# Cumulated forget logarithms as two rows of the forget attention's queries and keys; modulation sums two units earlier

## The chip, the cores and the metric

One core of one Trainium2 chip. The metric is the device time of one launch in microseconds (us); times of the kernel before are the median of several runs. One more execution was taken with the hardware profiler; all views come from that one.

## What is computed

Two transformer blocks, one after the other, on 256 tokens of width 1024 in float32. The first puts 16 meta tokens ahead (272 in all), and runs a SwiGLU feed-forward, a mixer of two attentions with 8 heads each, and a second feed-forward. The second block (modulated by a vector `c`) runs a gated linear attention beside a convolution, and then a layer that picks 16 of 16384 experts for each token and head and adds up their rows. The change lies in the second attention of the first block, the forget attention:

```python
def block_causal_attention(q, k, v, scale, key_valid, cum=None):
    ...
        s = jnp.einsum('bqhd,bkhd->bhqk', q[:, q0:q1], k[:, :q1]) * scale
        if cum is not None:
            cq = jnp.transpose(cum[:, q0:q1], (0, 2, 1))[:, :, :, None]
            ck = jnp.transpose(cum[:, :q1], (0, 2, 1))[:, :, None, :]
            s = s + (cq - ck)
    ...
    fq = rms_norm(fq[:, :, 0], g_q_fox)
    fk = rms_norm(fk[:, :, 0], g_k_fox)
    log_f = jax.nn.log_sigmoid(f_logit + b_forget)
    cum = jnp.cumsum(log_f, axis=1)
    o_fox = block_causal_attention(fq, fk, fv, 1.0 / math.sqrt(FOX_HEAD_DIM), key_valid, cum)
```

So the score of query t and key s of a head is scale * (q_t . k_s) + cum_t - cum_s. The second block needs its modulation vector, `silu(c) @ ada_w + ada_b`, a product with a matrix of 1024 x 6144.

## The kernel before

Each engine runs its own program in order, tied to the others by semaphores. SyncE (SP) loads the stream of weights in pieces of 1 MB into a ring of four (`load`, L578), loads the modulation matrix in 32 parts of 768 KB (`load_ada`, L585), and between them copies the experts' two tables side by side into one (`pair_up`, L592: two DRAM to DRAM copies of 512 KB a block, 128 blocks). `load_ada` waits until VectorE has done the sum two before it. 24 blocks are copied right after the last piece ahead of the second feed-forward; the last eight modulation loads come then, each followed by one block.

The modulation product is made by VectorE, in 32 sums `ada_add` (L1149, the work is L1153) of 128x1536. The last eight (parts 6 and 7 of `kt`) lie in the attention loop.

The mixer's projections end near 287 us. From then to 341 us the heads' queries and keys are normalised and rotated. The forget attention's queries lie in `fqz`, 128 rows for each of 8 heads, where an even head has its 64 rows in rows 0 to 63 and an odd one in rows 64 to 127; the other half is zero from a memset of VectorE (L1232). Its keys `fk` lie in pairs, two heads in 128 rows, so that a query with zeros in the other half picks its own. The forget logarithms of all heads lie in rows 96 to 103; VectorE cumulates them with a scan into `cumz` (L1283), zero in the other rows (L1229), and negates it into `ncumz` (L1285).

The attention runs over 32 units: 8 latent heads and then 8 forget heads, each in two tiles t of 128 queries. An even unit sees 144 keys (narrow), an odd one 272 (wide). TensorE works in the order `scores_of(n+2)`, `turn_probs(n)`, `weigh(n-1)`. In a forget unit `scores_of` has four products into one bank: queries and keys (L2006), `cumz` with a column of the constant `sel` that picks the head and divides by the scale (L2008), the same column with `ncumz` (L2009), and the causal mask (L2010). VectorE works in the order `soft_max(n+1)` (row maximum L1291, negated and scaled L1293), `scale_p(n)` (L1300, L1302), and behind every odd unit from 17 to 31 one `ada_add`. ScalarE does the exponential (L853), the copy of turned probabilities `probs_out(n-2)` (L767, L769) and the copy of the output `head_out(n-3)` (L777). Then comes the output product (L2056), a norm, the first half of the modulation sums' totals on TensorE (L1841), and the second feed-forward.

GpSimd splits weights for the feed-forwards (L666) and has nothing to do from 275 to 445 us.

Of the kernel before, what the change touches and what calls it, by code (L numbers as in the profile page):

```python
# [23 lines left out]
ALU = mybir.AluOpType  # L24
AX_X = mybir.AxisListType.X

P = 128
# [66 lines left out]
for _name, _n in VECS:  # L94
# [6 lines left out]
          ("ones", P), ("rot", P), ("cos", T), ("sin", T), ("neg_mask", P), ("iota", TOPK), ("sel", HEADS)]  # L101
# [9 lines left out]
def constants():  # L111
    c = np.zeros((P, N_CONSTS), np.float32)

    def put(name, a):
        at = CON[name][0]
        c[:a.shape[0], at:at + a.shape[1]] = a

    put("ident", np.eye(P, dtype=np.float32))
    for name, n in (("mean_d", D), ("mean_256", 256), ("mean_128", 128)):
        put(name, np.full((P, P), 1.0 / n, np.float32))  # L120
    put("mean_96", np.full((QK, QK), 1.0 / QK, np.float32))
    put("mean_64", np.kron(np.eye(2), np.full((HD, HD), 1.0 / HD)).astype(np.float32))
    put("ones", np.ones((P, P), np.float32))
    half = ROPE // 2
    rot = np.zeros((QK, QK), np.float32)
    for i in range(half):
        rot[NOPE + half + i, NOPE + i] = -1.0
        rot[NOPE + i, NOPE + half + i] = 1.0
    put("rot", rot)
    freq = (1.0 / (np.float32(10000.0) ** (np.arange(half, dtype=np.float32) / np.float32(half)))).astype(np.float32)  # L130
    ang = (np.arange(T, dtype=np.float32)[None, :] * freq[:, None]).astype(np.float32).astype(np.float64)
    cos = np.ones((QK, T), np.float32)
    sin = np.zeros((QK, T), np.float32)
    for at in (NOPE, NOPE + half):
        cos[at:at + half] = np.cos(ang)
        sin[at:at + half] = np.sin(ang)
    put("cos", cos)
    put("sin", sin)
    put("neg_mask", np.where(np.arange(P)[None, :] > np.arange(P)[:, None], NEG, 0.0).astype(np.float32))
    sel = np.zeros((P, HEADS), np.float32)  # L140
    for h in range(HEADS):
        sel[FL_ROW + h, h] = 1.0 / FOX_SCALE
    put("sel", sel)
    put("iota", np.broadcast_to(np.arange(TOPK, dtype=np.float32), (P, TOPK)))

    masks = np.zeros((P, len(LEVELS) - 1, 2, HD), np.uint32)
    s = np.arange(P)[:, None]
    for n, b in enumerate(LEVELS[:-1]):
        t = np.arange(P).reshape(-1, 2, b)[:, 1].reshape(1, HD)
        masks[:, n] = (s // b == t // b - 1)[:, None, :]  # L150
    return c, masks.reshape(P, -1)
# [27 lines left out]
def program(nc, a, out):  # L179
    ctx = ExitStack()  # L180
    with ctx:
# [96 lines left out]
        fk = view(HEADS // 2, T)  # L278
# [158 lines left out]
        cum_done = sem("cum_done")  # L437
        kpe_done = sem("kpe_done")
# [105 lines left out]
        NORM_COLS = [slice(0, T), slice(0, T), xc, xc, xc]  # L544

# [105 lines left out]
        def _(pool):  # L651
# [19 lines left out]
            for piece in range(BASE["w_in"] + 2, BASE["w_out"]):  # L671
                for e in range(2):
                    low(0, piece, piece % RING, e)
            each_piece(pool, BASE["ffn2"], FFN_P + 2, lambda piece, slot, turn: low(1, piece, slot, 1), peel=1)
# [26 lines left out]
        def _(act):  # L701
# [143 lines left out]

            units = 2 * HEADS * TT
            for n in range(units):
# [10 lines left out]
                if n >= 3:  # L858
                    head_out(n - 3)
            probs_out(units - 2)  # L860
# [229 lines left out]
        def _(dve):  # L1090
# [138 lines left out]
            then(dve.memset(cumz, 0.0), lb_step)  # L1229
            dve.wait_ge(half_used, half_number(0, BASE["w_out"], 0))  # L1230
            dve.tensor_scalar(km[pr, :, :], pe_all, V("g_k")[pr], None, ALU.mult).then_inc(kpe_done, 1)
            then(dve.memset(fqz[:, :, :], 0.0), lb_step)  # L1232
# [3 lines left out]
            dve.reciprocal(frms[0:N_META, 32:40], frms[0:N_META, 32:40]).then_inc(frec, 1)  # L1236
            for j in range(4):
# [6 lines left out]
            for j in range(4):  # L1244
                dve.wait_ge(fk_mm, j + 1)
                dve.scalar_tensor_tensor(fk[:, j, :], praw[:, 8 + j, :], V("g_fk"), ps[:, FK_BANKS[j], 0:T],
                                         ALU.mult, ALU.mult).then_inc(fox_done, 1)
# [35 lines left out]
            then(dve.tensor_tensor_scan(cumz[fr, :], C("ones")[fr, 0:1].broadcast_to([HEADS, T]), logf[fr, 3, :], 0.0,  # L1283
                                        ALU.mult, ALU.add), cum_done)
            dve.tensor_scalar(ncumz, cumz, -1.0, None, ALU.mult).then_inc(cum_done, 1)  # L1285
# [21 lines left out]
            for n in range(units):  # L1307
                if n + 1 < units:
                    soft_max(n + 1)
                scale_p(n)  # L1310
                if n % 2 and n >= units // 2:
                    ada_add(KT // 2 + n // 8, n // 2 % ADA_Q)
# [430 lines left out]
        def _(pe):  # L1743
# [174 lines left out]
            def fox_key(j):  # L1918

                if j:  # L1920
                    pe.wait_ge(fox_done, (4, 8, 9)[j - 1])
# [57 lines left out]
            pe.wait_ge(fox_done, 12)  # L1979
# [13 lines left out]
            def scores_of(n):  # L1993
# [8 lines left out]
                else:  # L2002
                    f = hd - HEADS
                    if f + t == 0:
                        pe.wait_ge(cum_done, 3)
                    pe.matmul(dst, fqz[:, f, q], fk[:, f // 2, 0:keys_n], start=True, stop=False)  # L2006

                    pe.matmul(dst, cumz[:, X0 + t * P:X0 + (t + 1) * P], C("sel")[:, f:f + 1].broadcast_to([P, keys_n]), start=False, stop=False)  # L2008
                    pe.matmul(dst, C("sel")[:, f:f + 1].broadcast_to([P, P]), ncumz[:, 0:keys_n], start=False, stop=False)  # L2009
# [423 lines left out]
```

## Time and profile before

| | us |
|---|---|
| median of 3 runs | 1688.76 |
| lowest and highest | 1685.34, 1688.95 |
| the profiled execution | 1678.1 |
| its span | 1676.3 |
| TensorE busy (matmul) | 1520.6 (91%) |
| VectorE busy | 1022.6 (61%) |
| ScalarE busy | 543.4 (32%) |
| GpSimd busy | 553.7 (33%) |

Of the chain that ended last, 70% of the span is TensorE's, 19% DMA's and 6% VectorE's. The profile's busy time of an engine says how much it worked; what ends a wait is read from the timeline, where the idle time before an instruction stands in brackets with what released it. A matmul in float32 is two instructions in the trace. "x2" means that two instructions are merged in one line. DMA share is that of the core's 16 DMA engines, and can read a little above 1.

### The profile page before, as it was taken

The page shows a single profiled execution, that of the slowest core. Times are in us where ns is not written, and L with a number is a line of the kernel's source. Part 1 is how long each engine was busy: PE and PEld are TensorE (multiplying, and loading weights), DVE is VectorE, ACT ScalarE, POOL GpSimd, SP SyncE. Part 2 cuts the span into 40 slices and gives each one's busy share as a digit, 9 for nine tenths or more (in the row PEclk, how much of TensorE's full clock was granted, in tenths as well). Part 3 has the DMA queues.
Part 4 walks back from the last instruction along what each step waited for, and adds up shares of the span by engine and source line. Part 5 has one row for each costly group of instructions (what it writes and reads, how often), then busy time and mean ns, then how long its engine had stood idle before and what let it go on. Part 6 is the DMA issues. An engine that isn't in the chain of part 4 may idle for free.

```text
span 1676.3 us, 22779 instructions
## 1 busy us (share of the span) xinstructions
PE 1520.6 (91%) x8260; PEld 1163.9 (69%) x8260; DVE 1022.6 (61%) x2102; ACT 543.4 (32%) x1101; POOL 553.7 (33%) x361
## 2 busy tenths in 40 slices
PE   6999989999999999999999997979987778778887
PEld 6999988778899999998889986534433333233333
DVE  5554355556343425998984845767676776767556
ACT  4443353353344335443115442212121212121213
POOL 3555444000144442001001412544554444354451
PEclk9999999899999998999999999999999989898999
DMA  7667699977789997998976839899999999999996
GB/s 270 242 221 254 234 349 384 327 261 264 296 316 374 368 366 285 363 370 322 331 260 238 318 109 376 326 426 426 427 427 426 428 427 426 427 428 426 427 427 273
DMA packets 98868, 571.87 MB, mean 341 GB/s; under 512 B 10976, under 2 KB 11104, under 8 KB 49120
## 3 DMA queue, kind: packets, MB, share of 16 engines
q1 hardware_dynamic: 60768, 298.15, 48.9%
q0 software_dynamic: 36864, 268.45, 38.1%
q10 hardware_dynamic: 1152, 4.17, 0.6%
q8 instruction: 50, 0.82, 0.2%
q14 instruction: 34, 0.28, 0.0%
HBM read 569.68 MB, written 135.27 MB: 421 GB/s over the span
## 4 chain that ended last, share of the span: by engine, by line
PE 70%; DMA 19%; DVE 6%; issue 2%; ACT 2%; another core or an unknown queue 1%; POOL 0%; ACTq 0%; POOLq 0%; DVEq 0%
DMA arena<-pairs,eidx 17%; PE ps L2299 12%; PE ps L1760 9%; PE ps L1762 9%; PE ps L1761 9%; PE ps L2105 5%; PE ps L1811 2%; PE ps L1813 2%; PE ps L1812 2%; PE ps L2269 2%; DMA ring<-pairs,eidx 2%; PE ps L2056 2%; PE ps L2122 2%; DVE arena L1639 1%; PE ps L1775 1%
## 5 line engine op out<-in xcount | busy, mean ns | idle before, releaser
L2299 PE MATMUL ps<-arena 128*128 128x512 f32 x872 | 421.1, 635 | 88.4 <-ACT arena L1059 88.1
L2299 PEld LDWEIGHTS ps<-arena 128*128 128x128 f32 x872 | 173.3, 203 | 321.8 <-issue 203.1
L1639 DVE CUSTOM_DVE_ANT_0 arena<-arena 128x1024 f32<-128x1024 f32 x218 | 265.4, 1223 | 165.9 <-DMA arena<-pairs,eidx 165.7
L666 POOL TENSOR_TENSOR w_lo<-ring,w_hi 128x1024 fp32r<-128x1024 f32 x82 | 217.6, 2656 | 427.0 <-DVE w_lo L1143 347.5
L696 POOL DMA_INDIRECT arena<-pairs,eidx x218 | 251.1, 1152 | 293.0 <-PE ps L2299 240.5
L1760 PE MATMUL ps<-u_hi,w_hi 128*128 128x256 f32 (+1 forms) x1056 | 305.1, 289 | 10.1 <-DVE u_lo L1112 10.0
L1762 PE MATMUL ps<-u_hi,w_lo 128*128 128x256 f32 (+1 forms) x1056 | 303.3, 287 | 0.0
L1761 PE MATMUL ps<-u_lo,w_hi 128*128 128x256 f32 (+1 forms) x1056 | 303.0, 287 | 0.0
L713 ACT ACTIVATE w_hi<-ring 128x1024 fp32r<-128x1024 f32 x188 | 197.9, 1056 | 170.3 <-PE ps L1813 77.5
L1760 PEld LDWEIGHTS ps<-u_hi,w_hi 128*128 128x128 f32 x1056 | 201.6, 191 | 12.7 <-issue 10.8
L1762 PEld LDWEIGHTS ps<-u_hi,w_lo 128*128 128x128 f32 x1056 | 202.4, 192 | 0.0
L1761 PEld LDWEIGHTS ps<-u_lo,w_hi 128*128 128x128 f32 x1056 | 201.5, 191 | 0.0
L1059 ACT ACTIVATE arena<-con,arena 128x128 f32<-128x128 f32 x256 | 82.8, 391 | 211.2 <-DVE arena L1660 199.7
L1143 DVE TENSOR_TENSOR w_lo<-ring,w_hi 128x1024 fp32r<-128x1024 f32 x70 | 85.9, 1228 | 83.4 <-ACT w_hi L713 83.4
L1053 ACT ACTIVATE arena<-arena 128x4 f32<-128x4 f32 (+1 forms) x73 | 15.0, 206 | 273.9 <-DVE arena L1639 273.8
L2299 PE MATMUL ps<-ring,arena 128*128 128x512 f32 x152 | 80.8, 658 | 20.4 <-ACT arena L1059 20.4
L1360 DVE SCALAR_TENSOR_TENSOR arena<-arena,cols 128x256 f32<-128x256 f32 x240 | 98.3, 477 | 0.0
L1166 DVE TENSOR_TENSOR arena<-arena,ps 128x272 f32<-128x272 f32 (+1 forms) x44 | 18.9, 429 | 126.5 <-PE ps L1762 126.5
L1811 PE MATMUL ps<-glu_hi,w_hi 128*128 (+2 forms) x320 | 91.0, 284 | 2.8 <-DVE glu_lo L1170 2.8
L1813 PE MATMUL ps<-glu_hi,w_lo 128*128 (+2 forms) x320 | 90.9, 284 | 0.0
L1812 PE MATMUL ps<-glu_lo,w_hi 128*128 (+2 forms) x320 | 90.8, 284 | 0.0
L2105 PE MATMUL ps<-u,ring 128*128 128x256 f32 x384 | 86.7, 384 | 1.3 <-PE ps L2105 1.3
(330 smaller groups left out, 2322.5 us busy)
## 6 DMA issues: line engine op xcount, KB each, us to landing
ring<-in_stream SPq DMA_DIRECT2D x130, 1024.0 KB, 6.8
pairs<-in_peer_u SPq DMA_DIRECT2D x128, 512.0 KB, 7.6
pairs<-in_peer_v SPq DMA_DIRECT2D x128, 512.0 KB, 8.6
arena<-in_ada SPq DMA_DIRECT2D x32, 768.0 KB, 6.3
arena<-pairs,eidx POOLq DMA_INDIRECT x218, 17.0
h<-in_x_t SPq DMA_DIRECT2D x1, 1088.0 KB, 7.4
arena<-in_keys ACTq DMA_DIRECT2D x1, 1024.0 KB, 7.3
con<-in_con ACTq DMA_DIRECT2D x1, 860.0 KB, 7.6
```

The lines of the kernel that those rows point to most:

```text
L666: pool.tensor_tensor(lo[:, half, :], ring[:, slot, e * HALF:(e + 1) * HALF], hi[:, half, :], ALU.subtract).then_inc(used if e else lo_done, 1)
L696: pool.indirect_dma_start(slot_of(n), None, pairs, bass.IndirectOffsetOnAxis(ap=eidx[:, n:n + 1], axis=0)).then_inc(landing(n)[0], 16)
L713: act.activation(w_parts(k)[0][:, half, :], ring[:, slot, e * HALF:(e + 1) * HALF], ACT.Copy).then_inc(hi_done, 1)
L1639: dve.tensor_tensor_reduce(row, row, hf[:, n % HEAD_ROWS // TOPK, :], 1.0, 0.0, ALU.mult, ALU.add, dots[:, n % HEAD_ROWS:n % HEAD_ROWS + 1 ...
L1760: pe.matmul(dst, hi[:, half, block], x[0][:, b, 0:w], start=(b == 0), stop=False)
L1761: pe.matmul(dst, hi[:, half, block], x[1][:, b, 0:w], start=False, stop=False)
L1762: mm = pe.matmul(dst, lo[:, half, block], x[0][:, b, 0:w], start=False, stop=(b == KT - 1))
L1811: pe.matmul(ps[:, m, 0:w], w_hi[:, half, block], hi, start=first, stop=False)
L1812: pe.matmul(ps[:, m, 0:w], w_hi[:, half, block], lo, start=False, stop=False)
L1813: mm = pe.matmul(ps[:, m, 0:w], w_lo[:, half, block], hi, start=False, stop=False)
L2105: mm = pe.matmul(ps[:, GATE_BANKS[i % 3], 0:SEQ], blk(slot, e * KT + b), u[:, b, 0:SEQ], start=(b == 0), stop=(b == KT - 1))
L2299: mm = pe.matmul(ps[:, Y_BANKS[j // TOPK] + half, :], diag[:, n % DIAGS, :], slot_of(n)[:, D + half * 512:D + half * 512 + 512], start=(hd ...
```

## The change

The two selector products of each forget unit go away. Instead the queries of a head get two more rows, cum/scale and 1, and its keys the rows 1 and -cum/scale, so that the one product of queries and keys also gives the difference of the logarithms.

- An even head uses rows 0 to 65 (its 64 and the two), an odd one all 128 (rows 0 and 1 beside its rows 64 to 127). Keys no longer lie in pairs: `fk` has a slot for each head, and the four evictions of 128 rows become eight of 64.
- GpSimd sets `fqz` to zero and the lower half of odd heads' keys, and then the extra rows of both to one (6 memsets, counted by `fox_set`), once the projections' weights are used. VectorE's memsets of `fqz` and `cumz` go away; it waits for `fox_set` before it writes queries.
- VectorE's scan goes to a scratch row block; two scalings write cum/scale and -cum/scale, for 8 rows.
- ScalarE issues, in each of units 3 to 10, two DMAs (`cum_rows`): one row of 256 and one of 272 numbers, from the logarithms' rows to the head's query and key rows. Before the first forget unit TensorE waits for all 16 (`cum_in`) where it waited for the scaled logarithms.
- The eight modulation sums come behind units 15 to 29 where they came behind 17 to 31, in the same order.

```diff
-          ("ones", P), ("rot", P), ("cos", T), ("sin", T), ("neg_mask", P), ("iota", TOPK), ("sel", HEADS)]
+          ("ones", P), ("rot", P), ("cos", T), ("sin", T), ("neg_mask", P), ("iota", TOPK)]
...
-        fk = view(HEADS // 2, T)
+        fk = view(HEADS, T)
...
+        CUM_ROWS = [slice(HD, HD + 2), slice(0, 2)]
+        FOX_ROWS = [slice(0, HD + 2), slice(0, 2 * HD)]
...
+            pool.wait_ge(half_used, half_number(0, BASE["w_out"], 0))
+            pool.memset(fqz[:, :, :], 0.0).then_inc(fox_set, 1)
+            pool.memset(fk[0:HD, 1::2, :], 0.0).then_inc(fox_set, 1)
+            pool.wait_ge(fox_set, 2)
+            for e in range(2):
+                pool.memset(fqz[CUM_ROWS[e], e::2, :], 1.0).then_inc(fox_set, 1)
+                pool.memset(fk[CUM_ROWS[e], e::2, :], 1.0).then_inc(fox_set, 1)
...
+            def cum_rows(hd):
+
+                row = CUM_ROWS[hd % 2].start
+                of = slice(FL_ROW + hd, FL_ROW + hd + 1)
+                act.wait_ge(fox_set, 6)
+                act.wait_ge(cum_done, 4)
+                act.dma_start(fqz[row:row + 1, hd, :], cumz[of, xc]).then_inc(cum_in, 16)
+                act.dma_start(fk[row + 1:row + 2, hd, :], ncumz[of, :]).then_inc(cum_in, 16)
...
+                if 3 <= n < 3 + HEADS:
+                    cum_rows(n - 3)
...
-            then(dve.memset(cumz, 0.0), lb_step)
...
-            then(dve.memset(fqz[:, :, :], 0.0), lb_step)
...
+            dve.wait_ge(fox_set, 6)
...
-                dve.scalar_tensor_tensor(fk[:, j, :], praw[:, 8 + j, :], V("g_fk"), ps[:, FK_BANKS[j], 0:T],
-                                         ALU.mult, ALU.mult).then_inc(fox_done, 1)
+                for e in range(2):
+                    r = slice(HD * e, HD * e + HD)
+                    dve.scalar_tensor_tensor(fk[r, 2 * j + e, :], praw[r, 8 + j, :], V("g_fk")[r], ps[r, FK_BANKS[j], 0:T],
+                                             ALU.mult, ALU.mult).then_inc(fox_done, 1)
...
-            then(dve.tensor_tensor_scan(cumz[fr, :], C("ones")[fr, 0:1].broadcast_to([HEADS, T]), logf[fr, 3, :], 0.0,
+            then(dve.tensor_tensor_scan(logf[fr, 1, :], C("ones")[fr, 0:1].broadcast_to([HEADS, T]), logf[fr, 3, :], 0.0,
                                         ALU.mult, ALU.add), cum_done)
-            dve.tensor_scalar(ncumz, cumz, -1.0, None, ALU.mult).then_inc(cum_done, 1)
+            dve.tensor_scalar(cumz[fr, :], logf[fr, 1, :], 1.0 / FOX_SCALE, None, ALU.mult).then_inc(cum_done, 1)
+            dve.tensor_scalar(ncumz[fr, :], logf[fr, 1, :], -1.0 / FOX_SCALE, None, ALU.mult).then_inc(cum_done, 1)
...
-                if n % 2 and n >= units // 2:
-                    ada_add(KT // 2 + n // 8, n // 2 % ADA_Q)
+                if n % 2 and units // 2 - 1 <= n < units - 1:
+                    i = (n - units // 2 + 1) // 2
+                    ada_add(KT - 2 + i // ADA_Q, i % ADA_Q)
...
-                    pe.wait_ge(fox_done, (4, 8, 9)[j - 1])
+                    pe.wait_ge(fox_done, (4, 8, 10)[j - 1])
...
-            pe.wait_ge(fox_done, 12)
+            pe.wait_ge(fox_done, 16)
...
-                        pe.wait_ge(cum_done, 3)
-                    pe.matmul(dst, fqz[:, f, q], fk[:, f // 2, 0:keys_n], start=True, stop=False)
-
-                    pe.matmul(dst, cumz[:, X0 + t * P:X0 + (t + 1) * P], C("sel")[:, f:f + 1].broadcast_to([P, keys_n]), start=False, stop=False)
-                    pe.matmul(dst, C("sel")[:, f:f + 1].broadcast_to([P, P]), ncumz[:, 0:keys_n], start=False, stop=False)
+                        pe.wait_ge(cum_in, 2 * HEADS * 16)
+                    own = FOX_ROWS[f % 2]
+                    pe.matmul(dst, fqz[own, f, q], fk[own, f, 0:keys_n], start=True, stop=False)
```

## Rows read from the trace of the kernel before

**Rows 1.** Stretches: width, busy (instructions) of each engine, granted clock, DMA share, GB/s.

```profile
350.00:369.70 19.70, 19.44 (x117) 15.02 (x116) 10.02 (x43) 12.20 (x51) 0.00 (x0) 1.00 0.84 306
366.00:368.00 2.00, 1.95 (x13) 1.42 (x13) 1.02 (x5) 1.86 (x9) 0.00 (x0) 1.00 0.43 176
369.70:409.70 40.00, 40.00 (x249) 33.85 (x248) 27.05 (x72) 17.78 (x81) 0.00 (x0) 1.00 0.73 262
550.00:600.00 50.00, 48.63 (x411) 48.43 (x411) 17.34 (x27) 19.38 (x22) 20.36 (x10) 1.00 1.00 372
```

**Rows 2.** Timeline of latent units: start, duration, engine, line, shapes, [idle before <- releaser].

```profile
355.13 0.71 PE L2034 MATMUL ps<-arena 128*128 128x128 f32 x4
357.18 0.44 DVE L1291 TENSOR_REDUCE arena<-ps 128x1 f32<-128x272 f32 x1 [1.25 <-PE ps L2010]
358.81 0.31 DVE L1291 TENSOR_REDUCE arena<-ps 128x1 f32<-128x144 f32 x1 [0.54 <-PE ps L2010]
359.04 0.52 PEld L2034 LDWEIGHTS ps<-arena 128*128 128x128 f32 x4 [0.34 <-ACT arena L769]
361.08 0.44 DVE L1291 TENSOR_REDUCE arena<-ps 128x1 f32<-128x272 f32 x1 [1.25 <-PE ps L2010]
```

**Rows 3.** Timeline of forget units, and the start of the output product.

```profile
376.00 0.31 DVE L1291 TENSOR_REDUCE arena<-ps 128x1 f32<-128x144 f32 x1 [1.09 <-PE ps L2010]
376.87 1.81 DVE L1153 SCALAR_TENSOR_TENSOR arena<-arena,silu_c 128x1536 f32<-128x1536 f32 x1
378.87 0.44 DVE L1291 TENSOR_REDUCE arena<-ps 128x1 f32<-128x272 f32 x1 [0.18 <-PE ps L2010]
408.82 0.44 DVE L1291 TENSOR_REDUCE arena<-ps 128x1 f32<-128x272 f32 x1 [0.18 <-PE ps L2010]
...
414.24 1.13 PE L2056 MATMUL ps<-arena,ring 128*128 128x256 f32 x4 [0.36 <-ACT arena L777]
```

**Rows 4.** Chain that ended last, narrow and wide forget unit: start, duration, what.

```profile
380.24 0.25 PE ps L2008 x2
380.49 0.24 PE ps L2009 x2
...
382.69 0.46 PE ps L2008 x2
383.14 0.46 PE ps L2009 x2
```

**Rows 5.** Modulation loads (L590): issues and landing at 346 to 352; all at 340 to 420.

```profile
L590 SPq DMA_DIRECT2D arena<-in_ada x2: 1104/1160/1217, 345.7 to 350.4; - x2
DMA to landing us min/median/max: 19.2/19.3/19.5
...
arena<-in_ada SPq DMA_DIRECT2D x8, 768.0 KB, 6.7
```

**Rows 6.** ScalarE's queue: an issue, the activation ahead of it, two transfers' KB and landing.

```profile
225.84 0.45 ACTq L790 DMA_DIRECT2D arena<-in_wuk  x1
226.24 0.47 ACT L745 ACTIVATE rstd<-ps,eps 128x272 f32<-128x272 f32 x1
...
masks<-in_masks ACTq DMA_DIRECT2D x1, 448.0 KB, 10.5
out<-arena ACTq DMA_DIRECT2D x1, 256.0 KB, 2.4
```

**Rows 7.** Timeline of SyncE: its last issue before 378 us.

```profile
352.63 2.53 SPq L597 DMA_DIRECT2D pairs<-in_peer_v  x1
```

**Rows 8.** VectorE before the attention (timeline), and GpSimd's memset of 128x2048 (its line).

```profile
301.24 4.07 DVE L1241 SCALAR_TENSOR_TENSOR arena<-arena,cols,ps 64x256 f32<-64x256 f32 x8 [6.54 <-PE ps L1908]
309.53 0.69 DVE L1256 TENSOR_TENSOR arena<-ps,con 96x512 f32<-96x512 f32 x1 [1.12 <-PE ps L1944]
342.36 0.30 DVE L1285 TENSOR_SCALAR arena<-arena 128x272 f32<-128x272 f32 x1
...
L677 POOL MEMSET arena<- x1: 1811/1811/1811, 650.7 to 650.7; 128x2048 f32 x1
```

More of the change, by code:

```diff
@@ L139, in constants @@
     put("neg_mask", np.where(np.arange(P)[None, :] > np.arange(P)[:, None], NEG, 0.0).astype(np.float32))
[L140 to L143, printed above, removed]
     put("iota", np.broadcast_to(np.arange(TOPK, dtype=np.float32), (P, TOPK)))
@@ L437, in program @@
         cum_done = sem("cum_done")
+        fox_set = sem("fox_set")
+        cum_in = sem("cum_in")
         kpe_done = sem("kpe_done")
```

## The prediction

> **What bounds the kernel now.** First the busy time by stretch [rows 1]. The change touches the attention, 341 to 414 us. In the forget heads (369.7 to 409.7) TensorE is busy all 40.00 us, and it was busy 19.44 of 19.70 us in the latent heads before them. Then the timeline, for what ends last.
>
> In the latent heads [rows 2] a pair of units takes 3.90 us (wide row maxima of L1291 at 357.18 and 361.08). VectorE waits 1.25 us for the mask matmul L2010, and TensorE waits 0.34 us for ScalarE's copy before L2034. So it is a loop of waits, wide maximum, exp, copy of turned probabilities, weighing (359.04 - 357.18 = 1.86), then scores of the unit four on and its maximum (357.18 - 355.13 = 2.05): 3.91 us, the pair.
>
> In the forget heads [rows 3] the pair takes (408.82 - 378.87) / 6 = 4.99 us. The wide maximum waits only 0.18 us, the narrow one at 376.00 waits 1.09, TensorE never waits: TensorE sets the pace. With it each pair holds a modulation sum, 1.81 us of VectorE (L1153), that costs nothing today.
>
> Behind the attention a shift passes on. The first product, L2056, starts at 414.24 on ScalarE's last copy [rows 3]. The second feed-forward is TensorE's (48.63 of 50 us busy at 550 to 600), though DMA stands at 1.00 beside it [rows 1]; its transfers are released by used weights and move with it. The transfers tied to the attention end with it. I take the shift as passed on whole.
>
> **The change, part by part.**
>
> *Removed: two matmuls in each of 16 units.* In a narrow unit L2008 and L2009 hold 0.25 + 0.24 us of the chain, in a wide one 0.46 + 0.46 [rows 4]: 1.41 us a pair, 11.3 us over eight. TensorE would need 4.99 - 1.41 = 3.58 us a pair. That is less than the latent heads' 3.91, so TensorE stops being the bound, and not all of the 11.3 us can come.
>
> *What is late next.* Three loops. (a) The wait loop above, 3.91. The key matmul has as many columns as the latent one and its rows lie in parallel (one of 66 rows bounds nothing below it), so it stays. (b) VectorE through the sum: narrow maximum to the sum's end, 376.87 + 1.81 - 376.00 = 2.68, and 0.02 to the next wide maximum, 2.70; from that to the weighing 1.86; from the weighing through wide scores, turn, narrow weighing and narrow scores to the narrow maximum 358.81 - 355.13 = 3.68 [rows 2, 3]. That is 8.24 us and spans two pairs: 4.12 a pair. The same in another way: the latent heads leave 1.25 us before the wide maximum where the sum needs 1.81. (c) The sums' weights from DMA, below. I take (b).
>
> *Timeline.* The sums now begin behind unit 15 and end behind unit 29. Without the selector matmuls the narrow maximum of unit 16 comes three pairs after 358.81, at 370.51 [rows 2], the sum runs behind it, and the wide maximum of unit 17 starts at 373.21. Seven pairs of 4.12 bring the maximum of unit 31 to 402.05. From it to L2056 is latency, 414.24 - 408.82 = 5.42 (today's last sum runs beside it), so L2056 starts at 407.47: **6.77 us** earlier. The data of the first two sums were asked for at 345.7 and 350.4 and land 19.2 to 19.5 us later [rows 5], by 365.2 and 369.6, in time for sums at about 371.4 and 375.5.
>
> *DMA under the sums.* A load waits for the sum two before it. From the end of that sum: 0.2 us to the issue, 6.7 to landing (median, [rows 5]), 1.81 for the sum, 8.7 us where two pairs at 4.12 give 8.24. Three such trips are +1.4 us. Lower bound nothing: a load that finds DMA idle lands sooner, and DMA is idle before the first of them. Upper bound by throughput: 0.73 of 40.0 us of full DMA [rows 1] for six loads and their copies is 4.87 us a pair, and seven pairs of 4.87 for 4.12 are +5.2. The backlog starts empty, so I stay near the landing row: **+1.2**.
>
> *ScalarE's 16 copies*, two in each of units 3 to 10. An issue from its queue took 0.45 us [rows 6], 0.9 a unit, 1.8 a pair. ScalarE is busy 12.20 of 19.70 us there, 2.42 a pair, and 2.42 + 1.8 is 0.3 over 3.91; four pairs make 1.2. But that issue at 225.84 ran while the activation ahead of it in the program, L745, started only at 226.24: issues run beside queued activations. If all do, it costs nothing. Queued behind the issues are the next exponential and copies, and TensorE waits for those. **+0.2**, range 0 to 1.2 while issue takes 0.45.
>
> *Their landing.* The unit of the maximum at 358.81 is the tenth; its issues are done near 360.6. TensorE needs them for unit 16's scores, near 369.7; behind that wait stand the turn of unit 14 and the weighing of unit 13. There are 9.1 us. Transfers from ScalarE's queue landed after 2.4 us with DMA quiet and 10.5 with four large loads in flight [rows 6]; SyncE's took up to 19.5 us behind their own queue [rows 5]. Stall: 0 to 10.4. SyncE's last issue before 378.9 is that of 352.63, and at 366 to 368 DMA is at 0.43 [rows 1, 7], so the copies meet draining queues: **0**.
>
> The Trainium skill ("DMA: Bandwidth & Descriptors", Issuing engines are not separate DMA queues) says that transfers from all issuing engines run on the same 16 DMA engines and that another issuer saves only issue time. It speaks against reckoning with a fast lane for ScalarE. Fully applied, with SyncE's slowest landing, it would add the 10.4 us; the rival below works that out from rows. The trace agrees in part, since masks took 10.5 us for less data than a stream piece.
>
> *GpSimd and VectorE.* VectorE loses a memset of queries and one of sums, in time it now waits away (6.54 us before L1241), and gets one small scaling before the first maximum, 0.30 like L1285 [rows 8]: **+0.3**, on the path. GpSimd zeroes the queries in 1.81 [rows 8], half the keys and four blocks of ones have about half as many columns each, so under 1 each: at most 7 us from 287. VectorE needs it at 301.24 and TensorE later still: nothing; GpSimd's next work is at 445. Key evictions become eight of 64 rows for four of 128, at 4.07 / 8 = 0.51 each. Between 305.31 and 309.53 there are 4.2 us for 4.07 [rows 8]; TensorE waits for the tenth, ready before it asks. Nothing, at worst 0.5. The clock cannot rise above the 1.00 of [rows 1], so there is no hidden gain there.
>
> *Sum:* 6.77 - 1.2 - 0.2 - 0.3 = **5.1 us** less.
>
> **The rivals.**
>
> *The sums' loads set the pace* (4.87 us a pair). For: the share above, and the 19.5 us that a load takes once queues are full [rows 5]. Against: the backlog starts empty. 6.77 - 5.2 - 0.5 = 1.1 us less: 1687.7.
>
> *The copies land late, the slower one.* If they queue like SyncE's, the last lands at 360.6 + 19.5 = 380.1, TensorE stands 10.4 us before unit 16: 5.3 us slower, 1694.1. It decides from 17.6 us of landing on (9.1 + 5.1 + 3.4). A kin of it: issues held for 2.53 us as SyncE's at 352.63 [rows 7] while queues are full, two a unit, ending the cover of ScalarE until 355. Against both: ScalarE's own rows, 0.45 and 10.5 us with four loads in flight [rows 6].
>
> *The change doesn't do what it says:* the pace stays near 5 because something I hold for free (bank waits, the copies) already stood there: no change, 1688. Or loop (b) is softer than its rows and the pair stays 3.91: 1.5 us more, 1682.2, within the forecast.
>
> **How the numbers follow.** The profiled execution took 1678.1 us, 1.8 around a span of 1676.3; the median of the runs is 1688.76, 0.6% above it. The absolute saving of 5.1 gives 1673.0 for a profiled execution and **1683.7** for the median. About 0.2%, 3.4 us, is what a measurement of this kernel tells from no change. Forecast (3 to 7 us less) 0.60; loads set the pace 0.22; late copies 0.12, of it 0.07 beyond 3.4 us; no effect 0.06. The forecast is near the border and the median of a few runs is uncertain by over 1 us, so 0.04 of it counts as the same: faster 0.58, same 0.35, slower 0.07. Range 1679.5 to 1690.5: below, the whole 6.8 us and an uncertain median; above, loads and ScalarE at their upper bounds and a late copy of about 2 us.
>
> **What would show it.** Right: L2008 and L2009 gone, wide maxima 4.1 us apart in units 17 to 31, VectorE with no wait before the wide maximum, TensorE waiting 0.5 us a pair, L2056 near 409, the latent heads' pair still 3.9, no wait of TensorE before unit 16. Wrong: L1153 waiting on the modulation load (the first rival), a gap before the first L2006 (the second), latent pairs of over 4.2 us (issues hold ScalarE), granted clock at half in the forget heads, which would double TensorE's 3.58 us, or L2056 earlier by 5 and the end not.

## The result, and the profile after

The changed kernel is **slower by 0.6%**: 1694.1 us (median of 11 runs) against 1685.67 for the kernel before on the same chip; ratio 1.0062, 95% interval 1.0041 to 1.0083. The forecast was 5.1 us less. Two of the eleven executions of the changed kernel were slow ones (1725.6 and 1726.1 us); every ratio in this text leaves such executions out, and it need not be the quotient of the medians beside it. The profiled execution took 1693.72 us over a span of 1691.9, where the one before took 1678.1 over 1676.3: 15.6 us more. That is more than the 10 us of the ratio: the eleven executions of before lie in two groups, four from 1679.1 to 1679.5 us and seven from 1685.3 to 1689.5, and the profiled one is even a little below the first. Where the 15.6 us arose is read below.

Line numbers of after: row maximum L1313 (L1291 before), modulation sum L1173 (L1153), mask matmul L2031 (L2010), output product L2077 (L2056), the feed-forward's totals L1864 (L1841), gather L705 (L696).

**Attention.** Stretches of after, for [rows 1] (columns as there), and then narrower ones:

```profile
350.00:369.70 19.70, 19.49 (x116) 15.03 (x117) 9.87 (x40) 12.44 (x54) 0.00 (x0) 1.00 0.90 322
369.70:409.70 40.00, 38.19 (x200) 29.43 (x199) 29.74 (x78) 19.53 (x88) 0.00 (x0) 0.87 0.75 282
550.00:600.00 50.00, 48.63 (x411) 48.43 (x411) 18.06 (x30) 19.75 (x24) 21.35 (x9) 1.00 1.00 367
```

```profile
390.00:392.00 2.00, 2.00 (x15) 1.64 (x13) 1.97 (x3) 0.00 (x0) 0.00 (x0) 1.00 1.07 430
392.00:394.00 2.00, 1.38 (x9) 0.84 (x8) 1.28 (x7) 1.80 (x9) 0.00 (x0) 1.00 1.05 399
396.00:398.00 2.00, 1.46 (x9) 0.89 (x8) 1.86 (x9) 1.24 (x6) 0.00 (x0) 1.00 1.01 396
398.00:400.00 2.00, 2.00 (x10) 1.52 (x10) 0.66 (x2) 0.85 (x5) 0.00 (x0) 0.77 1.01 415
400.00:402.00 2.00, 2.00 (x9) 1.58 (x8) 1.93 (x5) 0.26 (x1) 0.00 (x0) 0.50 1.05 426
416.00:418.00 2.00, 2.00 (x7) 1.55 (x6) 0.00 (x0) 0.00 (x0) 0.00 (x0) 0.50 0.00 0
418.00:420.00 2.00, 2.00 (x7) 1.66 (x6) 0.00 (x0) 0.00 (x0) 0.00 (x0) 0.61 0.00 0
420.00:422.00 2.00, 2.00 (x11) 1.74 (x11) 0.42 (x1) 0.00 (x0) 0.00 (x0) 1.00 0.00 0
```

TensorE has gaps (1.38 and 1.46 us busy of 2.00) and then runs at half of its clock, 1.2 for 2.4 GHz, from 399 to 419. Before, it was at 1.00 throughout the attention. The timeline of VectorE and of the output product, for [rows 3], shows what made the gaps:

```profile
374.59 0.43 DVE L1313 TENSOR_REDUCE arena<-ps 128x1 f32<-128x272 f32 x1
376.76 1.81 DVE L1173 SCALAR_TENSOR_TENSOR arena<-arena,silu_c 128x1536 f32<-128x1536 f32 x1
378.49 0.43 DVE L1313 TENSOR_REDUCE arena<-ps 128x1 f32<-128x272 f32 x1
...
385.07 1.82 DVE L1173 SCALAR_TENSOR_TENSOR arena<-arena,silu_c 128x1536 f32<-128x1536 f32 x1 [0.25 <-DMA arena<-in_ada]
386.80 0.43 DVE L1313 TENSOR_REDUCE arena<-ps 128x1 f32<-128x272 f32 x1
...
389.76 1.82 DVE L1173 SCALAR_TENSOR_TENSOR arena<-arena,silu_c 128x1536 f32<-128x1536 f32 x1 [0.86 <-DMA arena<-in_ada]
391.50 0.43 DVE L1313 TENSOR_REDUCE arena<-ps 128x1 f32<-128x272 f32 x1
...
394.37 1.82 DVE L1173 SCALAR_TENSOR_TENSOR arena<-arena,silu_c 128x1536 f32<-128x1536 f32 x1 [0.98 <-DMA arena<-in_ada]
396.11 0.43 DVE L1313 TENSOR_REDUCE arena<-ps 128x1 f32<-128x272 f32 x1
...
399.35 1.82 DVE L1173 SCALAR_TENSOR_TENSOR arena<-arena,silu_c 128x1536 f32<-128x1536 f32 x1 [1.34 <-DMA arena<-in_ada]
401.08 0.43 DVE L1313 TENSOR_REDUCE arena<-ps 128x1 f32<-128x272 f32 x1
...
407.06 0.44 DVE L1313 TENSOR_REDUCE arena<-ps 128x1 f32<-128x272 f32 x1 [0.94 <-PE ps L2031]
...
415.22 9.30 PE L2077 MATMUL ps<-arena,ring 128*128 128x256 f32 x32 [0.36 <-ACT arena L786]
```

The wide maxima of units 17 to 31 start at 374.59, 378.49, 382.57, 386.80, 391.50, 396.11, 401.08 and 407.06. Pairs take 3.90 and 4.08 us; then, as four sums wait for their data (0.25, 0.86, 0.98 and 1.34 us), 4.23, 4.70, 4.61 and 4.97; then 5.98 at half clock. The output product starts at 415.22 (414.24 before) and is busy 30.7 us for 28.6, since its first 4 us run at half clock. The totals start at 450.1 (447.0 before). Of these 3.1 us, 1.4 stand at the first wide maximum already (344.49 for 343.05), ahead of the attention loop. Counted from there, the output product starts after 70.7 us (71.2 before), where the forecast took 5.4 us off (6.77 - 1.2 - 0.2), and the totals after 105.6 (103.9).

**The last stage.** A stretch of the experts' gather, first of after and then of before, which was left out of the rows ahead of the prediction:

```profile
1200.00:1300.00 100.00, 79.14 (x179) 34.04 (x178) 69.41 (x188) 18.05 (x52) 44.93 (x41) 0.93 1.01 420
```

```profile
1200.00:1300.00 100.00, 80.39 (x176) 34.44 (x176) 70.69 (x191) 18.74 (x55) 47.51 (x41) 0.91 1.01 427
```

DMA is full in both (share 1.01), but moves 420 for 427 GB/s. No line of the diff lies in this stage. Its matmuls (L2320, L2299 before) start at 1049.9 (1045.1 before), and from there to the end of the span it takes 642.0 us for 631.2: **10.8 us** of the 15.6. Of the other 4.8, 3.1 stand at the totals already and 1.7 come on the way.

### The profile page after: what moved, and what is told of

It is laid out like the page before. It is cut to its first block, busy times and chain, and to the rows that moved or that the text cites. A ratio compares the mean times of both kernels' runs of the same rounds, so it can differ in the third digit from the quotient of the medians.

```text
span 1691.9 us, 22683 instructions
## 1 busy us (share of the span) xinstructions
PE 1527.5 (90%) x8196; PEld 1163.7 (69%) x8196; DVE 1024.0 (61%) x2105; ACT 543.7 (32%) x1101; POOL 549.1 (32%) x367
## 4 chain that ended last, share of the span: by engine, by line
PE 69%; DMA 20%; DVE 6%; issue 2%; ACT 2%; another core or an unknown queue 1%; POOL 0%; ACTq 0%; POOLq 0%; DVEq 0%; SPq 0%
DMA arena<-pairs,eidx 14%; PE ps L2320 12%; PE ps L1783 9%; PE ps L1785 9%; PE ps L1784 9%; PE ps L2126 5%; DMA ring<-pairs,eidx 5%; PE ps L1834 2%; PE ps L1836 2%; PE ps L1835 2%; PE ps L2290 2%; PE ps L2077 2%; PE ps L2143 2%; PE ps L1798 1%; DVE arena L1662 1%
## 5 line engine op out<-in xcount | busy, mean ns | idle before, releaser
L2320 PE MATMUL ps<-arena 128*128 128x512 f32 x872 | 426.5, 642 | 89.2 <-ACT arena L1079 89.2
L2320 PEld LDWEIGHTS ps<-arena 128*128 128x128 f32 x872 | 175.1, 205 | 326.0 <-issue 205.2
L705 POOL DMA_INDIRECT arena<-pairs,eidx x218 | 237.5, 1089 | 310.3 <-PE ps L2320 261.5
L2320 PE MATMUL ps<-ring,arena 128*128 128x512 f32 x152 | 80.2, 654 | 25.9 <-ACT arena L1079 25.9
```

The lines of the kernel that those rows point to most:

```text
L705: pool.indirect_dma_start(slot_of(n), None, pairs, bass.IndirectOffsetOnAxis(ap=eidx[:, n:n + 1], axis=0)).then_inc(landing(n)[0], 16)
L2320: mm = pe.matmul(ps[:, Y_BANKS[j // TOPK] + half, :], diag[:, n % DIAGS, :], slot_of(n)[:, D + half * 512:D + half * 512 + 512], start=(hd ...
```

## The experiments

Ratios are those of the time to the kernel before on the same chip (medians near 1682 us for the first two sets), over 12 executions each. Executions of one kernel spread by 10 us and more. One part arises ahead of the attention: the first wide maximum lies at 343 to 345 us in ten of the profiles and at 348 to 349 in four, and in these four, two of them of kernels with nothing changed ahead of it, TensorE's clock is at 0.50 to 0.56 from 340 to 350 us. The kernel before, and then the same with 56 unused columns (below), whose first maximum is at 348.44:

```profile
340.00:350.00 10.00, 8.21 (x53) 6.57 (x52) 7.00 (x26) 4.36 (x18) 0.00 (x0) 1.00 1.01 336
```

```profile
340.00:350.00 10.00, 9.20 (x37) 7.41 (x36) 5.16 (x17) 1.23 (x4) 0.00 (x0) 0.54 1.02 311
```

Another part arises behind it: from the totals to the last stage's first matmul it takes 592 to 606 us in six kernels whose code is the same there. Local readings are therefore taken as distances within one profile: from the first wide maximum to the output product and to the totals, and from the last stage's first matmul to the end of the span.

**A table of constants shorter by 32 bytes.** The constants lie in SBUF ahead of the arena, into which the gather writes. Deleting `("sel", HEADS)` moves the arena 32 bytes down: by the sizes of the tiles, and by a first address that no view shows, from byte 80384 of each partition, a multiple of 256, to 80352, 224 above one. Four kernels, the first with eight unused columns in the place of `sel`:

```diff
-          ("ones", P), ("rot", P), ("cos", T), ("sin", T), ("neg_mask", P), ("iota", TOPK)]
+          ("ones", P), ("rot", P), ("cos", T), ("sin", T), ("neg_mask", P), ("iota", TOPK), ("pad", HEADS)]
```

> The changed kernel with eight unused columns put back into the constants, so that the arena starts at byte 80384 of a partition as before, and not at 80352. Theory A (address): the expert rows' gather in the last stage moved 420 GB/s instead of 427 because its destinations in the arena start 32 bytes off; here it moves 427 again, the stage is some 10 us shorter, and the whole is 3 to 5 us slower than the kernel before or level with it (the lost clock of the attention stays). Theory B (the clock fall and the waits in the attention make the whole loss): the padding does nothing, 8 to 10 us slower than before. Theory C (the gather's rate differs between executions, whatever the kernel): padding does nothing that is steady.

Measured: 1682.17 us, ratio 1.0013 (0.9987 to 1.0039).

The same chip ran the changed kernel as it is:

> The changed kernel as it is, for the comparison on the same chip: 0.6% slower than before (8 to 11 us) under every theory; gather at 420 GB/s under A and B; under C now and then 427.

Measured: 1694.25 us, ratio 1.0067 (1.0040 to 1.0095). Eight unused columns take 0.54% away by the two ratios, some 9 us (12.1 by the two medians). The kernel before, its arena moved by `("pad", 56)` to 224 above a multiple of 256:

> The kernel before with 56 unused columns more among the constants, nothing else: the arena starts at 80608, 224 bytes above a multiple of 256, the same place within 256 bytes as in the changed kernel. Theory A: gather at 420 GB/s and the whole 8 to 11 us slower than before. Theories B and C: no change.

Measured: 1687.67 us, ratio 1.0046 (1.0020 to 1.0072), somewhat less than the 8 to 11 us expected. And by `("pad", 16)` to 64 above:

> The kernel before with 16 unused columns more: the arena starts at 80448, a multiple of 64 bytes but not of 128 or 256. If the gather wants its destinations on 64 bytes, no change and 427 GB/s; if it wants 256 bytes, as slow as the shift by 224. Theories B and C: no change.

Measured: 1691.28 us, ratio 1.0048 (1.0023 to 1.0073). The same stretch in the three, padded after first, then before at 224 and at 64:

```profile
1200.00:1300.00 100.00, 79.74 (x176) 34.32 (x176) 71.03 (x191) 18.75 (x55) 47.18 (x40) 0.91 1.01 427
```

```profile
1200.00:1300.00 100.00, 80.00 (x174) 34.11 (x173) 70.09 (x189) 18.32 (x54) 45.93 (x39) 0.90 1.01 420
```

```profile
1200.00:1300.00 100.00, 80.06 (x176) 34.42 (x176) 69.88 (x185) 18.74 (x55) 44.85 (x40) 0.91 1.01 421
```

From its first matmul to the end of the span the stage takes 640.7 to 642.1 us in all five profiles with the arena off a multiple of 256 (the next experiment's is one of them), and 631.1 to 632.2 in all nine with the arena on one. The address alone, with none of the change's work, costs what the changed kernel lost in this stage. Every tile behind the constants moves with the arena; that it is the gather's destination that counts is inferred from where the rate falls. Of the Trainium skill ("DMA: Bandwidth & Descriptors", How a descriptor splits into AXI transactions) two statements bear on it: transfers are cut at multiples of 256 bytes, and one that starts between them costs beats for bytes that it doesn't use. The page tells this of what a transfer reads, and here it is the place written to that moved; the direction agrees. An estimate by that page, with a row of 8192 bytes as one transfer and in its beats of 32 bytes, is 263 for 256 beats at 224, 2.7%, where 420 for 427 GB/s is 1.6%; at 64 it is 258, 0.8%, where 421 is 1.4%. The sizes don't agree, and the measurement decides.

**Is half of 256 enough?** Before with `("pad", 32)`, the arena 128 above a multiple, and before with the other buffer of the gather, `ring`, moved from 128 above a multiple onto one:

> The kernel before with 32 unused columns more among the constants: the arena starts at 80512, a multiple of 128 but not of 256 bytes. If 256 bytes is the boundary, as with the shifts by 224 and by 64: gather at 420 to 422 GB/s and 0.4 to 0.5% slower. If 128 is enough: 427 GB/s and no change.

Measured: 1699.86 us against 1685.97, ratio 1.0076 (1.0054 to 1.0099), 422 GB/s in the stretch, more than the 0.4 to 0.5% expected. The stage takes 640.7 us, no longer than with the other shifts. 128 isn't enough.

> The kernel before with the same 128 bytes ahead of and behind the ring, nothing else: ring and arena on 256 bytes. 0 to 1.5 us faster than before, by the same reckoning; gather at 427 to 428 GB/s.

Measured: 1685.67 us, ratio 1.0004 (0.9978 to 1.0030), 427 GB/s. One gather in seven (38 of 256) goes to `ring`; an alignment gained there, 1.5 us by their share of some 10, can't be told from none (the stage takes 632.1 us).

**What halves the clock?** The arena is on a multiple of 256 in all of these (the changed kernels carry the pad), so the gather runs at 427. First one matmul, whose result nobody reads, in each unit from 22 on; it fills TensorE's gaps and leaves the waits as they are.

```diff
+                if n >= FILL_FROM:
+                    pe.matmul(ps[:, 7, 0:T], ident, C("cos"), start=True, stop=True)
```

> The changed kernel with the arena on its old address, and in each unit from 22 on one more matmul of 128x272 into a bank that nobody reads, 0.46 us a unit; the loads stay as they are and VectorE still waits for them. If the lost clock is what costs, the clock stays at 1.00, forget pairs still take 4.6 us at the end, the output product starts near 411 and takes 28.7 us instead of 30.6, and the whole is 2 to 4 us faster than the same kernel without the filler. If the waits for the loads are what costs, the filler gains nothing or loses up to 5 us.

Measured: 1676.33 us, ratio 0.9957 (0.9940 to 0.9974). The padded kernel's stretch 400 to 410, and then that of this one:

```profile
400.00:410.00 10.00, 10.00 (x36) 7.88 (x36) 6.83 (x16) 3.54 (x15) 0.00 (x0) 0.50 0.56 227
```

```profile
400.00:410.00 10.00, 9.02 (x52) 6.41 (x51) 6.34 (x16) 4.75 (x21) 0.00 (x0) 1.00 0.52 213
```

The sums wait much as with the pad alone (4.2 us in 5 places):

```profile
DVE arena L1174 <- DMA arena<-in_ada: 3.5, 4, 1.5
```

Yet the clock stays at 1.00 to 410, and more work makes the kernel faster. From first maximum to output product it takes 411.25 - 343.64 = 67.6 us, the padded one 416.14 - 344.66 = 71.5; the totals come 102.0 us behind the first maximum for 106.1. The clock fell because TensorE stood in gaps. The fall, with at most 0.7 us of shorter waits, is worth 3.9 us there. It isn't gone altogether. Behind the last sums this kernel has gaps too, and the clock is at half for some 3 us in the output product, which is busy 30.3 us and not the 28.7 expected:

```profile
406.00:408.00 2.00, 1.40 (x9) 0.90 (x8) 1.32 (x6) 1.46 (x7) 0.00 (x0) 1.00 0.01 2
412.00:414.00 2.00, 2.00 (x6) 1.62 (x5) 0.00 (x0) 0.00 (x0) 0.00 (x0) 0.50 0.04 8
```

The whole gained 0.56% by the ratios on two chips, and 4.3 us by the medians against the kernel without filler of the same chip (1680.6, two experiments on); 4 us of it are seen in the attention.

Then the cause of the gaps. Behind each modulation load SyncE's loop issues the copy of one of the experts' blocks (`pair_up`); here all eight are issued behind the eight loads.

```diff
                 for q in range(ADA_Q):
                     load_ada(kt + (KT // 2 + 2), q)
-                    for n in range(ADA_BLOCKS):
-                        pair_up(kt * (ADA_Q * ADA_BLOCKS) + (at + q * ADA_BLOCKS + n))
+            for n in range((KT // 2 - 2) * ADA_Q * ADA_BLOCKS):
+                pair_up(at + n)
```

> The changed kernel with the arena back on its old address, and the eight blocks that SyncE copies between the last modulation loads copied behind these loads instead. If the chain is: loads compete with copies, so VectorE waits for a load in front of L1173, so TensorE thins out and its clock halves, then here L1173 has no wait for DMA, forget pairs stay at 4.05 us, the clock stays at 1.00 through 400 to 420 us and the output product starts 5 to 6 us sooner than in the kernel before (near 408 us) and ends some 6 us sooner: the whole 4 to 7 us faster than before. If the clock falls from the thinner TensorE work of 4.05 us pairs by itself, it still falls and the whole is level with before.

Measured: 1674.26 us, ratio 0.9951 (0.9931 to 0.9970). No sum waits for data, the last wide maxima lie 27.84 us apart over seven pairs (3.98), and the clock is 1.00 through 430. The loads' time to landing, in after and then here, says why:

```profile
L591 SPq DMA_DIRECT2D arena<-in_ada x6: 333/340/342, 374.9 to 396.4; - x6
...
DMA to landing us min/median/max: 4.1/7.1/7.5
```

```profile
L591 SPq DMA_DIRECT2D arena<-in_ada x6: 332/333/333, 375.5 to 395.3; - x6
...
DMA to landing us min/median/max: 4.1/4.2/4.3
```

TensorE is busy 21.3 of the 22 us from 376 to 398, and its clock stays; with the waits on top it is busy 20.2 in after and 20.0 with the pad, and its clock falls. So the thinner work by itself isn't the cause. The output product starts 408.45 - 344.60 = 63.85 us behind the first maximum, 7.3 less than before (71.19). But the totals start only 3.5 sooner (100.4 for 103.9 us). ScalarE waits for the first feed-forward piece, which queues behind the blocks (22.6 us at the longest, 12.3 before), TensorE is busy 1.50 and 0.22 us in the two stretches of 2 us from 436 to 440, and the norm (L1798) runs at half clock for most of its time:

```profile
ACT w_hi L722 <- DMA ring<-in_stream: 25.5, 2, 22.6
...
439.78 5.41 PE L1798 MATMUL ps<-arena,con 128*128 128x256 f32 x16 [2.27 <-ACT arena L750]
```

Before, the same 16 matmuls took 3.69 us.

Sums kept where they had been, behind units 17 to 31:

```diff
-                if n % 2 and units // 2 - 1 <= n < units - 1:
-                    i = (n - units // 2 + 1) // 2
+                if n % 2 and n >= units // 2:
+                    i = (n - units // 2 - 1) // 2
```

> The changed kernel with the arena on its old address and the sums behind units 17 to 31, where they were: this part of the change undone. The first sum starts 4 us later, the loads take the same 4.6 us steps, so the last sum ends some 4 us later; waits of VectorE and the fall of the clock stay, a pair later. Expected 0 to 3 us slower than with the sums behind units 15 to 29. If the early sums were what makes the clock fall, this is faster by 3 to 5 us instead.

Measured: 1680.6 us, ratio 1.0014 (0.9986 to 1.0042). The sums still wait 4.2 us, 4 times, clock 0.50 from 400 to 420: the place of the sums decides nothing that these executions can tell.

And the kernel before with its sums two units earlier, the other part of the change alone:

> The kernel before with the sums behind units 15 to 29 and nothing else: TensorE sets the pace at 4.99 us a pair, so the loads arrive in time; no change of the whole within 0.1%, clock at 1.00 throughout the attention.

Measured: 1680.45 us, ratio 0.9997 (0.9970 to 1.0023), pairs of 4.99, clock 1.00. Alone, this part does nothing, since TensorE sets the pace there.

**Both repaired.** The kernel with the pad and all blocks behind the loads has both losses repaired already. Blocks behind the loads with `ring` moved onto a multiple of 256 too (128 bytes of padding on either side of it):

> The version with the eight blocks copied behind the sums' loads, and 128 bytes ahead of the ring and 128 behind it, so that ring and arena both start on a multiple of 256 bytes (the ring started 128 bytes above one until now). If a start off 256 bytes is what slows a transfer into SBUF, the 38 expert rows that go to the ring and the whole weight stream get faster: up to 1.6% of 38 of 256 rows' time, 1 to 1.5 us in the last stage, and little in the weight stages, which TensorE bounds. The whole 0.5 to 0.6% faster than the kernel before. If 128 bytes suffice for the ring, as fast as without (0.995).

Measured: 1679.26 us against 1685.97, ratio 0.9964 (0.9938 to 0.9989): no more than without it. And, with `ring` where it was, the blocks spread, one behind every second load and four at the end, so that the feed-forward piece comes sooner:

```diff
                     load_ada(kt + (KT // 2 + 2), q)
-                    for n in range(ADA_BLOCKS):
-                        pair_up(kt * (ADA_Q * ADA_BLOCKS) + (at + q * ADA_BLOCKS + n))
+                    if q % 2:
+                        pair_up(kt * 2 + (at + q // 2))
+            for n in range(4):
+                pair_up(at + 4 + n)
```

> This is the changed kernel with the eight unused columns back (arena on a multiple of 256 bytes) and with the eight block copies of the forget heads spread in another way: one behind every second modulation load, the last four behind all of them. Theory (the blocks copied between the modulation loads made the sums wait for data, the waits thinned TensorE's work and its clock fell to half; and where all eight blocks stood behind the loads, the first feed-forward piece came late behind them and gave the gain back): the sums of the forget heads don't wait for data (their wait was 4.2 us before, in 4 or 5 places), the wide maxima keep 3.9 to 4.1 us a pair up to 403, the granted clock is 1.00 from 340 to 430, the output product begins at about 408 (416 with the blocks between the loads), ScalarE waits for the first feed-forward piece by some 10 us less than the 22.6 of the kernel with all eight behind, and the feed-forward's totals start 3 to 4 us sooner than there (441 to 442 against 445.0); the whole is 0.5 to 0.7% faster than the kernel before. Rival (the blocks' order is without effect on the feed-forward piece, what follows is bound by something else): the totals start at 444 to 446 again and the whole is 0.4 to 0.5% faster, as with all eight behind. Rival (one block in two loads is still too much for the queue): sums wait again for 2 us or more, the clock falls, and the time is within 0.2% of the kernel before.

Measured: 1672.8 us against 1680.29, ratio 0.9968 (0.9947 to 0.9989). Two stretches of the forget heads, and two waits:

```profile
396.00:398.00 2.00, 1.81 (x12) 1.27 (x12) 1.66 (x6) 1.83 (x10) 0.00 (x0) 1.00 1.08 347
398.00:400.00 2.00, 2.00 (x13) 1.66 (x14) 1.93 (x5) 0.57 (x2) 0.00 (x0) 1.00 0.81 323
...
DVE arena L1175 <- DMA arena<-in_ada: 0.2, 1, 0.2
...
ACT w_hi L724 <- DMA ring<-in_stream: 17.8, 2, 13.2
```

The clock is 1.00 from 350 to 440, and the loads land after 5.2 us. Locally it did what was expected: first maximum 349.17, output product 412.49 (63.3 us behind it), ScalarE's longest wait 13.2 for 22.6 us, totals at 445.23, 96.1 us behind it against 100.4 with all blocks behind and 103.9 before. (The absolute times expected, 408 and 441, were missed by this execution's start, 4.6 us later than with all blocks behind: it is one of the four with half a clock from 340 to 350 us.) Of these 7.9 us the whole shows 5 to 8, and its ratio can't be told from that with all blocks behind. The 592 to 606 us that the unchanged stretch behind the totals takes are spread enough to hide such a difference; whether they do isn't settled.

## Why the prediction was wrong

Two steps failed. The term for DMA under the sums, 1.2 us, had the waits too small and left out what they do to TensorE's clock: of the 5.4 us that were to have come by the output product, 0.5 came. And the diff's first hunk, the shorter table of constants, was put at nothing without a reason, and cost 10.8 us in the last stage.

The median measured is to the digit the 1694.1 us of the rival of late copies. That is chance: the mechanism didn't occur, and the rival's 5.3 us stood on a median of 1688.76 from three executions, where eleven gave 1685.67. Step by step:

- **TensorE as the bound of the forget heads, and loop (b)**: right. Once L2008 and L2009 were gone, pairs took 3.90 and 4.08 us while data were in time, 3.98 in the mean with the blocks behind the loads, for 4.12 forecast. The saving to the output product was put at 6.77 - 0.2 and measured as 7.3 and 7.9 us where sums don't wait. The softer loop, a rival within the forecast, is nearer. Latent pairs stayed at 3.90, but for one of 3.93.
- **ScalarE's copies**: right. Issue and landing in after, for [rows 6], by their lines:

```profile
L861 ACTq DMA_DIRECT2D arena<-arena x8: 504/504/611, 348.1 to 361.7; - x8
...
DMA to landing us min/median/max: 4.7/5.6/6.3
...
L862 ACTq DMA_DIRECT2D arena<-arena x8: 611/765/1496, 348.8 to 362.3; - x8
...
DMA to landing us min/median/max: 5.3/6.2/6.5
```

  The last landed near 369, TensorE never waited for them, and their issue, dearer than the 0.45 of [rows 6], cost no pair in this execution. In others one latent pair took 4.4 us: +0.2 was a fair price.
- **GpSimd's memsets and the extra scaling**: right, 0.29 for 0.30 us (from the first statistics matmul at 288.18, 287.03 before, to the first maximum 56.31 us for 56.02, the new scaling L1307 of 0.29 at its end). Memsets took 0.9 to 2.2 us each, two of them behind the first over the "under 1" of the working, 8.9 in all where 7 were the bound, with nobody waiting:

```profile
288.40 1.88 POOL L677 MEMSET arena<- 128x2048 f32 x1 [12.40 <-PE ps L1903]
...
294.36 1.00 POOL L682 MEMSET arena<- 2x1088 f32 x1
...
343.69 0.29 DVE L1307 TENSOR_SCALAR arena<-arena 8x272 f32<-8x272 f32 x1
```

- **DMA under the sums, +1.2**: the term that failed in the attention. The waits came to 3.4 us in 4 places (4.2 with the pad), within the range given but about three times the term. The backlog did start empty (DMA at 0.05 from 372 to 374), but it filled: 0.98 and more from 378 to 402, the loads landing after 7.1 us (median) for the 6.7 reckoned with, and up to 7.5. The runs with the blocks' copies moved show that it was these (`pairs<-in_peer`) that kept the loads from landing in time: 4.2 us without them. So of the rivals it is "the sums' loads set the pace", with its 4.87 us a pair and its chance of 0.22, that the trace shows in the pairs of 4.70, 4.61 and 4.97. Its price, 1.1 us less in all, failed by the next step too.
- **The clock**: the step stopped at the wait. In a loop where TensorE is no longer the bound, a wait of a sum is a gap of TensorE, and behind the gaps its clock was at half from 399 to 419, worth 3.9 us by the filler. Waits and clock together took all but 0.5 of the 7.3 to 7.9 us by the output product, and the product's start at half clock cost 2.1 more. The fall stood among what would make the prediction wrong, with no price and no chance, and the step "The clock cannot rise above the 1.00 of [rows 1]" looked only for a gain.
- **"Behind the attention a shift passes on"**: in part. Up to the totals all 7.9 us passed on with the blocks spread, and 3.5 of 7.3 with all of them behind the loads, where the feed-forward's first piece came late. Behind the totals the spread of executions covers it.
- **What was missed altogether**: the shorter table of constants. The diff's first hunk, taken as no cost, moved the arena 32 bytes down, and the last stage lost 10.8 us. The working never asked which tiles lie behind a tile that changes its size.
- **A slip**: 0.60 less the 0.04 that counts as the same is 0.56, not the 0.58 stated for faster. Nothing hangs on it.

No term of the sum and no rival stood for the table of constants. With both losses repaired the kernel is 0.3 to 0.5% faster than before, some 5 to 8 us, which is the size that the working forecast for the change.

## What to carry to other kernels

When a change resizes anything in SBUF, work out where every tile behind it now begins, and keep the destinations of long gathers on a multiple of 256 bytes; 32 bytes cost this kernel's last stage 10.8 us, about as much as the 11.3 us of matmuls that were taken out. When a change takes work from a busy TensorE, look at what the next bound does to it: small waits spread over a loop can cost the clock, and here that cost as much again as the 3.4 to 4.2 us of waits. And when a stage gets shorter, move the transfers that were issued in its shadow, watching which transfer then becomes the last.

## What the runs showed that was not expected

- SBUF destinations of an 8 KB row gather at 64, 128 or 224 bytes above a multiple of 256 cost 1.2 to 1.6% of the rate (421, 422 and 420 GB/s for 427) and about 10 us of a stage of 631, with DMA's share at 1.01 in all.
- The granted clock fell to 0.50 behind two stretches of 1.38 and 1.46 us busy of 2.00 that lay 4 us apart, each with full ones beside it, and returned 20 us later. All four profiles of kernels whose sums waited and that had no filler show the fall, at 398 to 405 us; the three with the copies moved keep 1.00 there. One of these three has stretches of 1.52 and 1.64 us, 4 us apart; what exactly tips the clock isn't settled. An unread matmul of 272 columns in each late unit, of no use otherwise, put the fall off to 411 us, cut it to some 3 us, and made the kernel faster (ratio 0.9957 for 1.0013).
- Beside GpSimd's memsets VectorE's copy of 32 x 2176 took 1.92 to 2.12 us in the eight profiles of changed kernels for 1.28 in the six of before, and the scaling behind it 2.12 to 2.17 for 1.34 or 1.35.
- A copy of one row of 1 KB inside SBUF, issued by ScalarE, held it for 0.50 to 1.50 us and landed after 4.7 to 6.5, with DMA at 1.02 from 347 to 363.
